# The first attention's probabilities normalised by Pool, and modulation chunks moved to the start of each attention

## What is computed

```python
for i in range(2):                                   # first_block
    shift, scale, gate = split(silu(c) @ w_ada[i] + b_ada[i], 3)     # and the same with c_ctx
    u = h * (1 + scale) + shift
    y = mixer(u, uc)          # i = 0: mixer_a, also for the context; i = 1: mixer_b
    h = layer_norm(ALPHA * h + gate * y)
...
# second_block
sh1, sc1, gt1, sh2, sc2, gt2 = split(silu(c_2) @ w_mod + b_mod, 6)
u = (rms_norm(x) * (1 + sc1) + sh1) @ w_in           # q, k, v, ga, gb
x = x + gt1 * (concat(dilated_attention(q, k, v), conformer_conv(ga, gb)) @ w_out)
x = x + gt2 * hier_moe(rms_norm(x) * (1 + sc2) + sh2)
return rms_norm(x)
```

```python
p = softmax(concatenate([s_lat, s_ctx, s_sink]))[..., :-1]
o = p @ v ; y = (o * silu(g)) @ w_out
```

## Time and profile before

| | us |
|---|---|
| median of 3 runs | 1308.79 |
| lowest and highest | 1308.18, 1309.35 |
| the profiled execution, all | 1312.69 |
| its span | 1310.8 |

### The profile page before, as it was taken

One profiled execution on the slowest core, in us unless ns is written; L12 is line 12 of the kernel. 1 busy time (PEld: TensorE's weight loads), 2 busy tenths in 40 slices (PEclk: granted clock), 3 DMA queues, 4 the chain that ended last, 5 costly groups with the idle time before them and its releaser, 6 DMA issues.

```text
span 1310.8 us, 14514 instructions
## 1 busy us (share of the span) xinstructions
PE 1240.4 (95%) x5876; PEld 670.2 (51%) x5876; DVE 407.4 (31%) x977; ACT 282.0 (22%) x634; POOL 17.4 (1%) x27
## 2 busy tenths in 40 slices
PE   4999989999989999899899898899999999999997
PEld 2446436654465446666688457544444444444442
DVE  1211019941230000491319932212222222222223
ACT  0000118850130000471220332211111111111102
POOL 0000000000001000120000000000000000000000
PEclk9899999999989999999989879899999999999999
DMA  9921530035334231528614756397999999999994
GB/s 344 388 86 64 192 115 15 1 133 188 110 129 106 70 122 64 153 49 285 250 65 170 280 193 238 123 381 298 427 427 429 427 430 427 429 428 427 430 424 176
DMA packets 81900, 311.27 MB, mean 237 GB/s; under 512 B 17969, under 2 KB 18812, under 8 KB 69050
## 3 DMA queue, kind: packets, MB, share of 16 engines
q1 hardware_dynamic: 78384, 309.56, 60.5%
q10 hardware_dynamic: 3386, 0.86, 0.3%
q0 software_dynamic: 80, 0.15, 0.0%
HBM read 309.39 MB, written 1.17 MB: 237 GB/s over the span
## 4 chain that ended last, share of the span: by engine, by line
PE 74%; DMA 16%; DVE 5%; ACT 2%; issue 1%; SPq 1%; DVEq 0%
PE ps L594 23%; DMA ring<-in_w_exp_up 15%; PE ps L847 12%; PE ps L696 8%; PE ps L590 6%; PE ps L877 4%; PE ps L539 3%; PE ps L660 3%; PE ps L714 3%; PE ps L649 3%; PE ps L639 2%; PE ps L814 2%; PE ps L826 2%; DMA ring<-in_w_ada 2%; DVE soft L1238 1%; PE ps L548 1%
## 5 line engine op out<-in xcount | busy, mean ns | idle before, releaser
L594 PE MATMUL ps<-U,ring 128*128 128x256 f32 (+1 forms) x928 | 299.6, 485 | 9.4 <-ACT U L1004 4.4
L594 PEld LDWEIGHTS ps<-U,ring 128*128 128x128 f32 x928 | 179.3, 194 | 123.0 <-issue 104.4
L847 PE MATMUL ps<-ring,prob 128*64 128x512 f32 x976 | 217.6, 593 | 5.4 <-DMA ring<-in_w_exp_up 4.6
L847 PEld LDWEIGHTS ps<-ring,prob 128*64 128x64 f32 x976 | 71.2, 137 | 144.0 <-issue 131.2
L877 PE MATMUL ps<-ring,prob 128*64 128x512 f32 x512 | 113.4, 595 | 0.0
L696 PE MATMUL ps<-U,ring 128*128 128x256 f32 (+1 forms) x384 | 110.9, 451 | 0.0
L696 PEld LDWEIGHTS ps<-U,ring 128*128 128x128 f32 x384 | 72.7, 190 | 37.5 <-issue 31.0
L590 PE MATMUL ps<-ring,U 128*128 128x512 f32 (+1 forms) x224 | 83.1, 531 | 0.0
L1567 DVE TENSOR_TENSOR prob<-ps,prob 128x512 f32<-128x512 f32 x16 | 17.2, 1077 | 202.4 <-PE ps L847 202.4
L877 PEld LDWEIGHTS ps<-ring,prob 128*64 128x64 f32 x512 | 35.3, 137 | 66.7 <-issue 66.7
L814 PEld LDWEIGHTS ps<-bias,U 128*128 128x128 f32 x512 | 59.7, 195 | 15.0 <-issue 15.0
(11 more groups left out here) (206 smaller groups left out, 951.3 us busy)
## 6 DMA issues: line engine op xcount, KB each, us to landing
ring<-in_w_exp_gate SPq DMA_DIRECT2D x30, 2048.0 KB, 15.5
ring<-in_w_exp_down SPq DMA_DIRECT2D x30, 2048.0 KB, 12.2
ring<-in_w_exp_up SPq DMA_DIRECT2D x29, 2048.0 KB, 17.3
ring<-in_w_ada SPq DMA_DIRECT2D x12, 2048.0 KB, 14.6
ring<-in_w_mod SPq DMA_DIRECT2D x12, 2048.0 KB, 8.3
ring<-in_b_w_in SPq DMA_DIRECT2D x8, 2048.0 KB, 8.1
ring<-in_a_w_in SPq DMA_DIRECT2D x5, 2048.0 KB, 19.8
ring<-in_w_in SPq DMA_DIRECT2D x5, 2048.0 KB, 9.2
```

The source lines that it names most:

```text
L594: last = mm(ps[:, b, 0:wid], w[:, col:col + P], src[:, k, 0:wid], start=(k == 0), stop=(k == KT - 1))
L847: last = mm(ps[x * CAP:(x + 1) * CAP, 2 + i, :], xg[:, k, x * CAP:(x + 1) * CAP], chunk(n, 2 * i + x)[0][:, k, :], start=(k == 0), stop=(k ...
```

## The change

It has three parts.

1. In attention a, VectorE's `sums` ends with the reciprocal and signals a new semaphore, `share_ok`. Pool multiplies the two heads' probabilities of the unit by it, in place, and signals `prob`, which TensorE waits for. Attentions b and c keep the multiplication on VectorE.
2. `EARLY` chunks of the modulation (two of `ada1`, two of `mod_a`, three of `mod_b`) move into the attention: the streams between scores(1) and scores(2), the folds between scores(3) and P·V(0). ScalarE copies their rows between the second and the third exponentials. They get row buffers of their own (`rows_beside`) and columns in the upper half of bank 6. The streams write banks 6, 7 and 5, and TensorE's wait for `mod_ok` 7 ahead of c moves behind c. `take_mod2` for the first three chunks of `mod_b` moves behind attention c on VectorE.
3. The three attentions share one set of eight semaphores (`at`); each use adds the count of what the attentions before have signalled (`past`).

```diff
@@ gpsimd
+            for n, (p, kind, qb, kts) in enumerate(UN["a"]):
+                pool.wait_ge(share_ok, n + 1)
+                for x in range(2):
+                    pr = prob[:, n % AHEAD, x * T:x * T + len(kts) * P]
+                    last = pool.tensor_scalar(pr, pr, soft[:, n % 4, 4, x:x + 1], None, ALU.mult)
+                last.then_inc(at["prob"], 1)
+
             for p in range(NH // 2):
                 mask_bias(p)
@@ vector, sums
+                    if L == "a":
+                        v.reciprocal(s[:, 4, :], s[:, 2, :]).then_inc(share_ok, 1)
+                        return
                     step(v.reciprocal(s[:, 4, :], s[:, 2, :]))
                     settle()
@@ tensor, attention
-                for n in range(AHEAD):
+                for n in range(2):
                     scores(n)
+                for c in range(EARLY[stage]):
+                    stream(stage, c, (6, 7, 5)[c])
+                scores(2)
                 for n, (p, kind, qb, kts) in enumerate(un):
-                    pe.wait_ge(at[L, "prob"], n + 1)
+                    pe.wait_ge(at["prob"], past[L, "prob"] + n + 1)
...
                     if n + AHEAD < len(un):
                         scores(n + AHEAD)
+                    if n == 0:
+                        for c in range(EARLY[stage]):
+                            fold(stage, c, v0, nv, 6)
...
-            modulation("ada1", range(4), 0, 2, (4, 5), 6)
+            modulation("ada1", range(2, 4), 0, 2, (4, 5), 6)
...
-            modulation("mod_a", range(4), 2, 1, (4, 5), 6)
+            modulation("mod_a", range(2, 4), 2, 1, (4, 5), 6)
...
-            modulation("mod_b", range(3), 2, 1, (5, 6), 7)
-            pe.wait_ge(mod_ok, 7)
@@ scalar, attention
                 exps(0)
                 exps(1)
+                mod_rows(stage, range(EARLY[stage]), (6, 7, 5))
...
-            mod_rows("mod_b", range(3), (5, 6))
-            attention("c")
+            attention("c", "mod_b")
@@ vector
-            take_mod2(CHUNKS["mod_b"] + 3, 0, 24, 36, 7)
             attention("c", bias_c)
+            take_mod2(CHUNKS["mod_b"] + 3, S, 24, 36, 6)
```

## The result

The changed kernel took 1329.11 us (median of 4 runs, 1326.2 to 1329.44), the kernel before 1309.07 beside it. The ratio is 1.0144, with an interval of 1.013 to 1.0159: slower by some 20 us, on the side that was forecast, but with three times the forecast's +6.4. The profiled execution took 1329.44 with a span of 1327.5, which is 16.7 over the span of before.

The account below looks back on a forecast made before the run. Took TensorE (74% of the chain) as the bound, with TensorE and VectorE both full in attention a's four-tile steps. Attentions a +6.0, b -3.1, c +3.5 sum to +6.4 us: 1315, range 1302 to 1333.

Parts of the forecast that it names:

- the size of P: Length of one Pool normalisation instruction in attention a: 1.10 us for 512 columns, 0.75 for 256.
- The straight line: Pool price drawn through rows of 128 columns (0.61 us) and 384 (0.86): 0.74 for 256 columns, 0.99 for 512.
- the long steps: Attention a's four-tile steps: 3.44 us each (+0.26), 15 of them costing 3.9 us.
- the short ones: Attention a's two-tile steps: 2.30 us each (+0.28), 16 of them costing 4.5 us.
- The loop through Pool: Attention a: four-tile step 2.34 + P, two-tile step 1.55 + P; break-even at P = 0.84 and 0.47.
- The start with a clock that stays up: Start of attention a: Pool's 2.2 us and the folds make unit 0's P·V 3.3 us later.
- the chunks behind a: Modulation after attention a: two chunks remain of four, so the end of a is shorter by 5.7 us.
- b: Attention b: moved chunks fill TensorE's idle time at its start, -3.1 us, bounded by 0 and -5.7.
- c: Attention c: mask 1.74 us earlier, but three folds at the low clock delay P·V(0) by 3.7; +3.5 us.
- The rival of a quick Pool: Attention a: P of 0.63 and 0.31, under both break-evens; total -3.8, 1305 us; chance 0.17.
- The slow Pool: Rival, attention a: P of 2.43 and 1.22; a costs +38, total +39, 1347 us; chance 0.15.
- The clock high in c: Rival, attention c: TensorE's clock stays high, c gives -5.6, total -2.7, 1306 us; chance 0.20.

Follow-up runs that it names:

- kernel 5: kernel 1, but in attention a VectorE normalises head 0 and Pool head 1 with a TENSOR_TENSOR; 1312.35 us, ratio 1.0018.
- kernel 3: The whole change, but Pool multiplies both heads in one TENSOR_TENSOR with broadcast reciprocals instead of two TENSOR_SCALARs; 1308.82 us, ratio 0.9987.
- kernel 7: The whole change, but Pool multiplies by the constant 1.0 instead of the reciprocal, leaving attention a unnormalised; 1320.45 us (one run).
- kernel 1: The whole change without its Pool part: VectorE normalises in all three attentions, moved chunks and shared semaphores stay; 1305.82 us, ratio 0.9957.
- 4: The whole change plus five unused 512-column matmuls ahead of attention a's first turn, where TensorE waited for Pool; 1331.32 us, ratio 1.015.
- 8: The whole change, but Pool's 512-column instructions are each cut in two of 256; 1333.16 us, ratio 1.0177.
- 9: The whole change, but attention a's two folds stand ahead of unit 0's turn, in TensorE's wait for Pool; 1327.85 us, ratio 1.0131.
- kernel 2: The kernel before plus Pool's normalisation alone, with chunks and semaphores in their old places; 1335.92 us, ratio 1.0186.
- kernel 6: kernel 1, but attention c's folds stand ahead of scores(2) and ScalarE copies their rows ahead of its first exponentials; 1300.41 us, ratio 0.9938.
- 10: The whole change with the TENSOR_TENSOR of kernel 3 and the order of attention c of kernel 6; 1302.99 us, ratio 0.996.

## Why the prediction was wrong

**The step that failed** is the size of P: "I take 1.10 and 0.75, between them for the long one, at the line for the short one". It measured 1.57 and 0.92. The straight line went through a TENSOR_SCALAR at 128 columns and a TENSOR_TENSOR at 384, and these are two operations with different prices per column: 0.0025 us for the first (0.61, 0.92, 1.57), 0.0017 for the second (0.61, 1.04 for 256 and 512 in kernel 5). A line from the cheap point of the dear operation to a point of the cheap operation is flatter than either. Only the upper bound, the TENSOR_SCALAR's own time per column, came from the right operation, and because it counted the fixed cost as rate it lay too high (2.43 and 1.22). The measured values lie in between and inside the range's bound of 1.7 and 0.95.

What that is worth: the long steps rose by 0.63 (3.81 against 3.18) and not 0.26, 15 of them 9.4 us instead of 3.9; the short ones by 0.45 and not 0.28, 16 of them 7.2 instead of 4.5. With 0.9 for the first unit's Pool work at the start, this is 9 of the 17 us by which a was missed. That the whole was missed by less, 13.6 us by the medians and 10.3 by the profiled executions, is luck: c was missed by 5.0 the other way.

**The second miss** is TensorE's clock in a. The prediction gave the clock a term only in c; for a it had none, and it left "clock levels that fall elsewhere" out of its range. The fall at the start made P·V(0) late by 6.2 and not 3.3 (0.9 of it is P, the rest folds and scores at the low level); the fall at the end left 3.0 of the 5.7 that the two chunks should save (8.62 from the last P·V to the projection, against 11.64 before and 5.97 in kernel 3); and the steps behind both falls took some 3 more than P explains (99.3 from the first to the last P·V, against 79.6 + 16.6). Together that is about 8 us; the comparison with kernel 7 gives 6.6. How much the clock cost is read from these rows; why it fell stays open.

Point by point, the rest:

- *The loop through Pool* was right in form (2.25 + P measured for 2.34 + P forecast; in the two-tile step 1.55 + P, as forecast) and so was the statement that both engines were full, so that a freed VectorE gives nothing: kernel 3 has its Pool at the break-even and a is no faster than in kernel 1.
- *The start with a clock that stays up*: +2.9 in kernel 3 against +3.3; *the chunks behind a*: -5.7 there, as forecast.
- *b*: -3.4 against -3.1.
- *c*: counted from the convolution, P·V(0) came 2.8 later (3.7 forecast), and the folds ran at the low level, as forecast (5.28 for 5.4). The stage still gained 1.5 instead of losing 3.5. From P·V(0) to the projection the change took 27.5 us, where before took 31.8 and every other kernel 29.9 to 31.1. In the change the clock came up at 779, still within the attention, and in before it was 0.50 to 764 and up to nearly 769. Kernels 1, 3, 4, 5, 7, 8 and 9, with the same order in c, took 88.9 to 90.5, which is 1.1 to 2.7 *over* before, and kernel 2 took 86.2 with the order of before; so the forecast of a loss was nearer to the common case than the profiled execution of the change was. The stage goes with the time that the clock spends at the low level in it: 17.1 us in the change for a c of 86.3, 23.9 in 3 and 5 for 88.9, 27.3 in 4, 7 and 9 for 89.3, 30.7 in 1 and 8 for 90.4 and 90.5. What sets that time, no run here settles.
- *The rival of a quick Pool* fell with P; with it fell the "roughly line-rate" that the prediction cited from the Trainium skill (GPSIMD Engine Reference, 4.1 Engine selection): the trace shows 1.57 us on Pool where VectorE takes 0.48 to 0.50, with one tensor input. *The slow Pool* was right in direction, and its measured loss lies between it and the forecast. *The clock high in c* did not happen in the change, only its late rise.
- *The shared semaphores* were costed at nothing. They were never run alone. Two four-tile steps of a take 7.61 us in kernel 2, which has the old ones, and 7.62 in the change, and steps of b take 3.11 us before and in the change, so they cost nothing per step that shows.

## What to carry to other kernels

Price an instruction by rows of the same operation on the same engine only, at two sizes if there are two; where there is only one, take the whole time per column as the upper bound and weigh the forecast towards it, and look whether another operation of that engine does the same work for less. A step that is moved to another engine pays its length once per loop that runs through it, so write down that loop first and its break-even, and ask whether anything waits for the engine that is freed. Where narrow matmuls are moved into a stage, put them beside another engine's long work, as kernels 6 and 10 did, and not between a turn and its P·V. Read a stage together with its granted clock, in more than one execution.

## What the runs showed of the hardware that was not expected

- On Pool, in fp32 from SBUF to SBUF, a TENSOR_SCALAR took 0.61, 0.92 and 1.57 us on 128, 256 and 512 columns, and a TENSOR_TENSOR with a broadcast second input 0.61, 1.04 and 1.89 on 256, 512 and 1024. The operation with two inputs is the cheaper one. An immediate in place of the pointer saved 0.08.
- VectorE's TENSOR_SCALAR on 512 columns took 1.37 us beside a Pool instruction and 0.50 without one; it ended 0.28 behind Pool's. Once in 16 it was Pool's that was held, 1.33 for 1.04. VectorE operations with two SBUF inputs ran beside Pool's TENSOR_SCALAR at their usual 0.16 in 24 of 31 cases.
- TensorE's granted clock fell to the 1.2 GHz level at the start of a in the change and in kernels 1, 2, 7, 8 and 9, and not in 3, 4, 5, 6 and 10, with orders of work that differ little. What came ahead of a fall was a wait of 2.0 to 2.5 us without folds (the change, 2, 8), one of 1.9 and the folds (7), one of 0.7 and the folds (9), or the folds alone (1). It stays open what separates kernel 1 from kernel 6, which have the same order there.
